# Within a weight unit: all K tiles of the first output tile, high and low weights in turn, then those of the second

## The chip, the cores and the metric

One core of a Trainium2 chip runs the whole program. The metric is the device time of one execution in microseconds (us). The kernel before takes 2347.33 us (median of 3 runs, 2344.61 to 2349.43).

## What is computed

A two-layer encoder trunk on 256 tokens of width 2048, in float32. Nearly all of the work is matrix products of the 256 token vectors with large weight matrices:

```python
for layer in range(2):
    x = x + (attention_layer if layer == 0 else rglru_layer)(rms_norm(x, g), ...)  # projections in and out
    x = x + memory_cross_attention(rms_norm(x, xa_norm[layer]), memn, wq, wkv, ...)
    x = x + conv_ffn(rms_norm(x, ffn_norm[layer]), w_up, conv_w, conv_b, w_down)   # 2048 -> 11264, 5632 -> 2048
```

## The kernel before

**Number format.** A float32 product is made from parts that TensorE takes in its fp32r format. ScalarE writes the high part of each weight (`w_hi`, L301), and VectorE writes the rest (`w_lo`, L307). Activations are split the same way into `xg_hl` or `a_hl`, which hold, for every K tile of 128 rows, 256 high columns and then 256 low columns. Three of the four partial products are computed: high weight with high and low activation, and low weight with high activation.

**Weight stream.** All weights are read from memory in 788 units of 128 x 1024 numbers, in the order of use, by SyncE's queue. There are four slots of `raw`, `w_hi` and `w_lo`. TensorE starts a unit when its `w_lo` is written (semaphore `lo_done`), and its last matmul signals `pe_unit`, upon which the slot is written again and, at the end of a block, the sums in PSUM are read.

**The unit that the diff touches.** 672 of the 788 units are "pair units" (`pair_unit`, which calls `pair_part`): four K tiles by two output tiles of 128 features. They make up the output projections (sections out0, xo0, down0, out1, xo1, down1), the up projections (up0, up1) and the recurrent block's input projection (rec). A K tile with one output tile takes two matmuls. The high one (L332) has 512 moving columns, the activation's high and low halves side by side, and fills a PSUM bank of 512 float32 columns. The low one (L336) has 256 moving columns and adds into the bank's second half. The two output tiles m = 0 and m = 1 have a bank each, `bank + m`. A block (one pair of output tiles, all its K tiles) uses banks 0 and 1 or 2 and 3 in turn. It begins with a wait on `proj_free`, the signal that the block before the last one has been read out.

**Waits inside a unit.** In the sections that start before all their inputs are split, `ready(xk)` waits for K tile xk: `tile_there` in `out_section`, and in the first block of `up_section` and `rec_section`. In xo0 and xo1 the first two blocks are issued in halves of two K tiles (`pair_part` with `ks` of length two), block 0 and block 1 in turn.

**The other two forms of unit** are not touched. `feature_unit` (L317, cross-attention queries) issues, for each K tile, three matmuls of 256 moving columns into the same half of one bank. `token_unit` (L352, attention and memory projections) has the activation as the stationary operand. For each K tile it issues three matmuls of mostly 512 moving columns into one bank and then three into a second bank.

Of the kernel before, what the change touches and what calls it, by code (L numbers as in the profile page):

```python
# [16 lines left out]
P = 128  # L17
# [60 lines left out]
def trunk(nc, t):  # L78
# [3 lines left out]
    with ctx:  # L82
# [11 lines left out]
        def sb(name, shape, dt=F):  # L94
            o = top[0]
            top[0] += size(shape)
            return at(name, o, shape, dt)
# [10 lines left out]
        w_hi = sb("w_hi", [SLOTS, UE], R)  # L108
# [85 lines left out]
        ps = ctx.enter_context(nc.psum_tensor("ps", [P, 8, COLS], F))  # L194
# [57 lines left out]
        n = 0  # L252
# [38 lines left out]
        def times(k, i, per):  # L291
            return k if i is None else k + i * per
# [28 lines left out]
        def pair_part(pe, c, k0, ks, x, bank, start, stop, i=None, per=0, ready=None, done=True):  # L321

            s = c % SLOTS
            pe.wait_ge(lo_done, times(c + 1, i, per))
            for k in ks:
                xk = k0 + k - ks[0]
                if ready:
                    ready(xk)
                both = x[:, xk, :, :].rearrange("p a n -> p (a n)")
                for m in range(2):  # L330
                    w = slice((2 * k + m) * P, (2 * k + m + 1) * P)
                    nc.tensor.matmul(ps[:, bank + m, :], w_hi[:, s, w], both, start=start and k == ks[0],  # L332
                                     stop=False, skip_group_check=True)
                for m in range(2):
                    w = slice((2 * k + m) * P, (2 * k + m + 1) * P)
                    last = nc.tensor.matmul(ps[:, bank + m, SEQ:2 * SEQ], w_lo[:, s, w], x[:, xk, 0, :], start=False,  # L336
                                            stop=stop and k == ks[-1], skip_group_check=True)
            if done:
                last.then_inc(pe_unit, 1)

        def pair_unit(pe, c, k0, x, bank, start, stop, i=None, per=0, ready=None):
            pair_part(pe, c, k0, range(4), x, bank, start, stop, i, per, ready)
# [139 lines left out]
        def _(pe):  # L482
# [143 lines left out]
            def out_section(name, ready, scale, base):  # L626
# [15 lines left out]
                if name == "out1":  # L642

                    for x, (q, u) in enumerate(OUT1_ORDER):
                        if u == 0:
                            pe.wait_ge(proj_free, fblock[name] + q + 1)
                        pair_unit(pe, c0 + x, 4 * u, a_hl, 2 * q, u == 0, u == units - 1, ready=tile_there)
                    blocks(None, (2, 3))
                    blocks(1, range(4))
                elif units == 1:  # L650

                    for q in range(2):
                        pe.wait_ge(proj_free, fblock[name] + q + 1)
                    for k in (0, 2):
                        for q in range(2):
                            pair_part(pe, c0 + q, k, (k, k + 1), a_hl, 2 * q, k == 0, k == 2, ready=tile_there, done=k == 2)
                    blocks(None, (2, 3))
                    blocks(1, range(4))
                else:
                    with pe.Fori(0, 2) as i:  # L660
                        blocks(i, range(4))
# [1184 lines left out]
```

## Time and profile before

| | |
|---|---|
| median of three runs | 2347.33 us (2344.61 to 2349.43) |
| profiled execution, its own time | 2346.71 us |
| its span, first to last instruction | 2345.0 us |
| mean granted TensorE clock | 0.998 |
| TensorE matmul busy | 2302.9 us, 98%, 13036 matmuls |
| TensorE weight load busy | 1997.7 us, 85% |
| VectorE busy | 1588.4 us, 68% |
| ScalarE busy | 1238.7 us, 53% |

PE is TensorE's matmuls, PEld its weight loads, DVE is VectorE, ACT ScalarE, POOL GpSimd, SP SyncE. A matmul's duration in a profile reaches from its start to its last result, so durations of neighbours overlap. The time that a matmul costs in a stream is the distance from its start to the start of the next one.

### The profile page before, as it was taken

The numbers are of one execution on the slowest core, as the hardware profiler recorded it, in microseconds if no ns is written. First come the engines' busy times: TensorE is split into PE (matmuls) and PEld (weight loads), VectorE is DVE, ScalarE is ACT, GpSimd is POOL, SyncE is SP. The second block draws the span as 40 slices with busy tenths as digits, with TensorE's granted clock in tenths as the row PEclk, the third lists the DMA queues.
The fourth block names the chain that finished last, engine by engine and source line by source line (L and its number), as shares of the span: only waits on it lengthen the run. The fifth ranks groups of instructions, "written<-read, shape, count | busy, mean of one in ns | idle before, by whom it ended". The sixth has DMA issues, their size and how long they took to land.

```text
span 2345.0 us, 38374 instructions
## 1 busy us (share of the span) xinstructions
PE 2302.9 (98%) x13036; PEld 1997.7 (85%) x13036; DVE 1588.4 (68%) x1968; ACT 1238.7 (53%) x1692; POOL 221.7 (9%) x207
## 2 busy tenths in 40 slices
PE   7999999999999999999999999999999999999999
PEld 6888878978888888888888888887888888888888
DVE  7766776576777777765555778667777777774444
ACT  5554555465555555544444776555555555553332
POOL 6630001130000000000000100212000000000000
PEclk9999999999999999999999999999999999999999
DMA  7565435545555555565555555534555555556554
GB/s 277 175 199 197 135 106 178 180 132 163 193 185 183 188 200 181 180 210 189 189 187 186 180 189 187 181 138 149 202 184 179 194 191 188 183 189 201 189 188 160
DMA packets 118077, 426.92 MB, mean 182 GB/s; under 512 B 13504, under 2 KB 14144, under 8 KB 117872
## 3 DMA queue, kind: packets, MB, share of 16 engines
q1 hardware_dynamic: 116640, 418.36, 53.5%
q0 software_dynamic: 1360, 7.52, 0.9%
q8 instruction: 50, 0.82, 0.1%
q14 instruction: 27, 0.22, 0.0%
HBM read 423.73 MB, written 2.10 MB: 182 GB/s over the span
## 4 chain that ended last, share of the span: by engine, by line
PE 89%; POOL 4%; issue 3%; DVE 2%; ACT 1%; DMA 1%; POOLq 0%; SPq 0%; ACTq 0%; DVEq 0%
PE ps L332 50%; PE ps L336 25%; PE ps L352 9%; PE ps L317 1%; POOL acc L405 1%; POOL sq L404 1%; PE ps L592 1%; PE ps L758 1%; POOL acc L1703 0%; DVE w_lo L307 0%; DMA memT<-in_mem_t 0%; POOL acc L1704 0%; PE ps L577 0%; ACT w_hi L301 0%; POOL rq L1644 0%
## 5 line engine op out<-in xcount | busy, mean ns | idle before, releaser
L307 DVE TENSOR_TENSOR w_lo<-raw,w_hi 128x1024 fp32r<-128x1024 f32 x788 | 963.8, 1244 | 514.1 <-ACT w_hi L301 510.8
L301 ACT ACTIVATE w_hi<-raw 128x1024 fp32r<-128x1024 f32 x788 | 811.9, 1054 | 593.1 <-PE ps L336 437.7
L332 PE MATMUL ps<-xg_hl,w_hi 128*128 128x512 f32 x3328 | 1047.8, 396 | 5.4 <-DVE w_lo L307 4.5
L336 PEld LDWEIGHTS ps<-xg_hl,w_lo 128*128 128x128 f32 x3328 | 625.9, 188 | 148.0
L336 PE MATMUL ps<-xg_hl,w_lo 128*128 128x256 f32 x3328 | 654.6, 278 | 0.0
L332 PE MATMUL ps<-a_hl,w_hi 128*128 128x512 f32 x2048 | 644.9, 396 | 8.3 <-DVE xT L1388 4.7
L332 PEld LDWEIGHTS ps<-xg_hl,w_hi 128*128 128x128 f32 x3328 | 507.6, 189 | 6.3 <-issue 4.8
L336 PEld LDWEIGHTS ps<-a_hl,w_lo 128*128 128x128 f32 x2048 | 384.7, 188 | 91.0
L336 PE MATMUL ps<-a_hl,w_lo 128*128 128x256 f32 x2048 | 402.4, 278 | 0.0
L332 PEld LDWEIGHTS ps<-a_hl,w_hi 128*128 128x128 f32 x2048 | 311.8, 189 | 11.2 <-DVE xT L1388 7.2
L1040 ACT ACTIVATE y_buf<-u_buf,fconv 128x256 f32<-128x256 f32 x176 | 96.4, 595 | 228.0 <-DVE u_buf L1470 228.0
L352 PE MATMUL ps<-w_hi,xg_hl 128*128 128x512 f32 (+1 forms) x576 | 174.3, 382 | 11.5 <-DVE w_lo L307 11.5
L1477 DVE SCALAR_TENSOR_TENSOR y_buf<-u_buf,fconv,y_buf 128x256 f32<-128x256 f32 x176 | 85.2, 485 | 82.2 <-ACT y_buf L1040 81.6
L352 PEld LDWEIGHTS ps<-w_hi,xg_hl 128*128 128x128 f32 x576 | 106.8, 189 | 33.3 <-issue 13.4
L352 PE MATMUL ps<-w_lo,xg_hl 128*128 128x512 f32 (+1 forms) x288 | 109.2, 379 | 0.0
L1515 DVE TENSOR_TENSOR u_buf<-cross,ps 128x512 f32<-128x512 f32 x88 | 60.5, 687 | 44.9 <-ACT cross L1073 44.9
L352 PE MATMUL ps<-w_hi,a_hl 128*128 128x512 f32 x256 | 86.1, 402 | 0.9 <-ACT kmem_tok L877 0.6
L1035 ACT ACTIVATE a_hl<-y_buf 128x512 f32 (+1 forms) x44 | 27.8, 632 | 104.1 <-DVE y_buf L1499 104.1
L1482 DVE SCALAR_TENSOR_TENSOR y_buf<-u_buf,fconv,y_buf 128x256 f32<-128x256 f32 x176 | 77.0, 479 | 0.2
L352 PEld LDWEIGHTS ps<-w_lo,xg_hl 128*128 128x128 f32 x288 | 54.7, 190 | 9.8
L1470 DVE TENSOR_TENSOR u_buf<-u_buf,r_bc 128x512 f32<-128x512 f32 x88 | 60.3, 685 | 0.0
L1026 ACT ACTIVATE y_buf<-y_buf 128x512 f32<-128x512 f32 x44 | 27.8, 633 | 61.2 <-DVE y_buf L1482 61.1
(186 smaller groups left out, 1414.8 us busy)
## 6 DMA issues: line engine op xcount, KB each, us to landing
raw<-in_w_stream SPq DMA_DIRECT2D x788, 512.0 KB, 3.9
bias<-in_rel_bias POOLq DMA_DIRECT2D x4, 768.0 KB, 6.0
memT<-in_mem_t POOLq DMA_DIRECT2D x1, 2048.0 KB, 11.0
gate_w<-in_gate_w POOLq DMA_DIRECT2D x4, 512.0 KB, 3.8
out_t<-xT SPq DMA_DIRECT2D x8, 256.0 KB, 4.4
xT<-in_x_t SPq DMA_DIRECT2D x2, 512.0 KB, 8.7
xT<-in_x_t SPq DMA_DIRECT2D x2, 384.0 KB, 6.0
xT<-in_x_t SPq DMA_DIRECT2D x1, 256.0 KB, 4.0
```

Of the source, the lines that this page charges most:

```text
L301: nc.scalar.activation(w_hi[:, s, :], raw[:, s, :], ACT.Copy).then_inc(hi_done, 1)
L307: nc.vector.tensor_tensor(w_lo[:, s, :], raw[:, s, :], w_hi[:, s, :].bitcast(F), ALU.subtract).then_inc(lo_done, 1)
L332: nc.tensor.matmul(ps[:, bank + m, :], w_hi[:, s, w], both, start=start and k == ks[0], stop=False, skip_group_check=True)
L336: last = nc.tensor.matmul(ps[:, bank + m, SEQ:2 * SEQ], w_lo[:, s, w], x[:, xk, 0, :], start=False, stop=stop and k == ks[-1], skip_group_ ...
L352: last = nc.tensor.matmul(ps[:, bank + tt, 0:n], a[:, k0 + k, tok], b[:, s, w], start=start and k == 0 and q == 0, stop=stop and k == nk - ...
L1026: A(flat(y_buf[:, 2:4, :]), flat(y_buf[:, 2:4, :]), ACT.Gelu_apprx_tanh).then_inc(gelu_done, 1)
L1035: A(pair_tiles(a_hi, 2 * half, 2, i, 4), y_buf[:, 0:2, :], ACT.Copy).then_inc(g_hi, 1)
L1040: A(y_buf[:, m, :], u_buf[:, m, 2:2 + SEQ], ACT.Identity, scale=column(fconv, w + 2, i, 32), bias=column(fconv, w + 3, i, 32)).then_inc(ta ...
L1470: V.tensor_tensor(part, part, r_bc[:, :].unsqueeze(1).to_broadcast([P, 2, SEQ]), ALU.mult).then_inc(u_scaled, 1)
L1477: middle.append(ch.mark(V.scalar_tensor_tensor(y_buf[:, m, :], u_buf[:, m, 1:1 + SEQ], column(fconv, 4 * (4 * half + m) + 1, i, 32), y_buf ...
L1482: ins = V.scalar_tensor_tensor(y_buf[:, m, :], u_buf[:, m, 0:SEQ], column(fconv, 4 * (4 * half + m), i, 32), y_buf[:, m, :], ALU.mult, ALU ...
L1515: V.tensor_tensor(u_buf[:, tile:tile + 2, 2:2 + SEQ], cross[:, :, :], ps[:, bank:bank + 2, 0:SEQ], ALU.add).then_inc(proj_free, 1)
```

## The change

Before, a K tile's four matmuls go high m=0, high m=1, low m=0, low m=1, and then the next K tile follows. Afterwards all K tiles of the part are done for m=0 (high, low, high, low, ...) and then all of them for m=1. The matmuls, their operands and their number stay the same. `ready` is called in the first pass only. The last matmul of the unit is the same one as before, and it carries the same signal.

```diff
             pe.wait_ge(lo_done, times(c + 1, i, per))
-            for k in ks:
-                xk = k0 + k - ks[0]
-                if ready:
-                    ready(xk)
-                both = x[:, xk, :, :].rearrange("p a n -> p (a n)")
-                for m in range(2):
+            for m in range(2):
+                for k in ks:
+                    xk = k0 + k - ks[0]
+                    if ready and m == 0:
+                        ready(xk)
                     w = slice((2 * k + m) * P, (2 * k + m + 1) * P)
-                    nc.tensor.matmul(ps[:, bank + m, :], w_hi[:, s, w], both, start=start and k == ks[0],
-                                     stop=False, skip_group_check=True)
-                for m in range(2):
-                    w = slice((2 * k + m) * P, (2 * k + m + 1) * P)
+                    nc.tensor.matmul(ps[:, bank + m, :], w_hi[:, s, w], x[:, xk, :, :].rearrange("p a n -> p (a n)"),
+                                     start=start and k == ks[0], stop=False, skip_group_check=True)
                     last = nc.tensor.matmul(ps[:, bank + m, SEQ:2 * SEQ], w_lo[:, s, w], x[:, xk, 0, :], start=False,
                                             stop=stop and k == ks[-1], skip_group_check=True)
```

## Rows read from the trace of the kernel before

**Rows 1.** The page: span, and busy time of each engine.
```profile
span 2345.0 us, 38374 instructions
PE 2302.9 (98%) x13036; PEld 1997.7 (85%) x13036; DVE 1588.4 (68%) x1968; ACT 1238.7 (53%) x1692; POOL 221.7 (9%) x207
```
**Rows 2.** The page: chain that ended last, shares by line.
```profile
PE ps L332 50%; PE ps L336 25%; PE ps L352 9%; PE ps L317 1%; POOL acc L405 1%; POOL sq L404 1%; PE ps L592 1%; PE ps L758 1%; POOL acc L1703 0%; DVE w_lo L307 0%; DMA memT<-in_mem_t 0%; POOL acc L1704 0%; PE ps L577 0%; ACT w_hi L301 0%; POOL rq L1644 0%
```
**Rows 3.** The page: groups; busy, mean ns of one, idle before, releaser.
```profile
L307 DVE TENSOR_TENSOR w_lo<-raw,w_hi 128x1024 fp32r<-128x1024 f32 x788 | 963.8, 1244 | 514.1 <-ACT w_hi L301 510.8
L301 ACT ACTIVATE w_hi<-raw 128x1024 fp32r<-128x1024 f32 x788 | 811.9, 1054 | 593.1 <-PE ps L336 437.7
L332 PE MATMUL ps<-xg_hl,w_hi 128*128 128x512 f32 x3328 | 1047.8, 396 | 5.4 <-DVE w_lo L307 4.5
L336 PE MATMUL ps<-xg_hl,w_lo 128*128 128x256 f32 x3328 | 654.6, 278 | 0.0
L332 PE MATMUL ps<-a_hl,w_hi 128*128 128x512 f32 x2048 | 644.9, 396 | 8.3 <-DVE xT L1388 4.7
L336 PE MATMUL ps<-a_hl,w_lo 128*128 128x256 f32 x2048 | 402.4, 278 | 0.0
```
**Rows 4.** Waits of PE: total us, times, longest.
```profile
PE ps L332 <- DVE xT L1388: 5.6, 14, 0.7
PE ps L332 <- DVE w_lo L307: 4.5, 2, 2.3
...
PE ps L332 <- DVE a_hl L1588: 2.5, 1, 2.5
...
PE ps L332 <- DVE a_hl L1329: 1.1, 1, 1.1
```
**Rows 5.** Timeline of PE in up0, at 799 to 806 us: start, length.
```profile
799.69 0.63 PE L332 MATMUL ps<-xg_hl,w_hi 128*128 128x512 f32 x2
800.15 0.40 PE L336 MATMUL ps<-xg_hl,w_lo 128*128 128x256 f32 x2
800.39 0.63 PE L332 MATMUL ps<-xg_hl,w_hi 128*128 128x512 f32 x2
...
805.26 0.62 PE L332 MATMUL ps<-xg_hl,w_hi 128*128 128x512 f32 x2
```
**Rows 6.** The same stretch in narrow windows: single matmuls and weight loads.
```profile
799.92 0.39 PE L332 MATMUL ps<-xg_hl,w_hi 128*128 128x512 f32 x1
800.16 0.19 PEld L336 LDWEIGHTS ps<-xg_hl,w_lo 128*128 128x128 f32 x1
800.27 0.28 PE L336 MATMUL ps<-xg_hl,w_lo 128*128 128x256 f32 x1
```
**Rows 7.** Windows of PE: stretch, length, busy (matmuls), granted clock, DMA share, GB/s.
```profile
548.00:551.50 3.50, 3.50 (x12) 0.55 0.70 193
600.00:1000.00 400.00, 400.00 (x2298) 1.00 0.56 188
...
1650.00:2050.00 400.00, 400.00 (x2298) 1.00 0.56 189
```
**Rows 8.** Timeline of PE in the token units: first and last triple of eleven.
```profile
164.83 0.62 PE L352 MATMUL ps<-w_hi,xg_hl 128*128 128x512 f32 x2
165.28 0.39 PE L352 MATMUL ps<-w_lo,xg_hl 128*128 128x512 f32 x1
...
171.63 0.62 PE L352 MATMUL ps<-w_hi,xg_hl 128*128 128x512 f32 x2
```
**Rows 9.** Chain in order of time, in the feature units: start, length.
```profile
446.50 14.40 PE ps L317 x120
```
**Rows 10.** Timeline of PE at 547.9 us, after a wait for weights.
```profile
547.94 0.82 PE L332 MATMUL ps<-xg_hl,w_hi 128*128 128x512 f32 x2 [2.18 <-DVE w_lo L307]
548.56 0.63 PE L336 MATMUL ps<-xg_hl,w_lo 128*128 128x256 f32 x2
548.98 1.05 PE L332 MATMUL ps<-xg_hl,w_hi 128*128 128x512 f32 x2
549.84 0.63 PE L336 MATMUL ps<-xg_hl,w_lo 128*128 128x256 f32 x2
```
**Rows 11.** Timeline of DVE and PE where out0 starts.
```profile
356.25 1.29 DVE L1329 TENSOR_TENSOR a_hl<-oT,a_hl 128x512 fp32r<-128x512 f32 x2 [0.45 <-ACT a_hl L939]
357.09 0.69 PE L332 MATMUL ps<-a_hl,w_hi 128*128 128x512 f32 x2 [1.08 <-DVE a_hl L1329]
```
**Rows 12.** Timeline of DVE where xo0 and up0 start.
```profile
482.94 0.42 DVE L1436 TENSOR_TENSOR a_hl<-ps,a_hl 128x256 fp32r<-128x256 f32 x1 [0.93 <-ACT a_hl L992]
483.89 0.42 DVE L1436 TENSOR_TENSOR a_hl<-ps,a_hl 128x256 fp32r<-128x256 f32 x1 [0.53 <-ACT a_hl L992]
...
514.80 0.98 DVE L1158 SCALAR_TENSOR_TENSOR xg_hl<-xT,gains,xg_hl  x2
```
**Rows 13.** Timeline of PE where xo0 starts, its third block, and where up0 starts.
```profile
483.09 0.81 PE L332 MATMUL ps<-a_hl,w_hi 128*128 128x512 f32 x2
...
486.06 0.63 PE L332 MATMUL ps<-a_hl,w_hi 128*128 128x512 f32 x2
...
489.25 0.73 PE L332 MATMUL ps<-a_hl,w_hi 128*128 128x512 f32 x2 [0.24 <-DVE xT L1388]
...
510.12 0.73 PE L332 MATMUL ps<-xg_hl,w_hi 128*128 128x512 f32 x2 [0.45 <-DVE xT L1388]
```

## The prediction, made before the changed kernel was run

> **What bounds the kernel now.** I read the page's busy times first. Matmuls keep TensorE busy for 2302.9 of 2345.0 us, and the next engine, VectorE, has 1588.4 [rows 1]. Then I read the shares of the chain that ended last: three quarters of it are the two matmul lines that the diff reorders, L332 and L336 [rows 2]. The groups of the page show the same from the other side. The two engines that prepare weights stand idle for 514.1 and 593.1 us, and ScalarE's idle time ends mostly on L336, so the weights wait for TensorE and not the reverse [rows 3]. The idle time in front of L332 is 5.4 + 8.3 us, in front of L336 it is nothing [rows 3]; who ended it is in the waits, of which the largest is the readout of a block (L1388), 14 times and 5.6 us together [rows 4]. So the time is the number of matmuls times the distance between their starts. Only a change of that distance can move the total by much.
>
> **How many matmuls.** The diff reorders 3328 + 2048 = 5376 high matmuls and as many low ones [rows 3], 10752 together, 16 in each of the 672 pair units. A distance that changes by 0.1 ns per matmul is 1.1 us in the total. The bound for telling a change from none, 0.2%, is 4.7 us, which is 0.44 ns per matmul.
>
> **The distance now.** From 799.69 to 805.26 us eight K tiles start, 32 matmuls [rows 5]: 5.57 / 32 = 174.1 ns each, or 0.696 us for the four of a K tile. Two windows of 400 us agree, with 2298 matmuls each [rows 7]: 800 / 4596 = 174.1 ns. Within a K tile the starts are 799.69 (high), 799.92 (high), 800.15 (low), 800.27 (low), 800.39 (the next high) [rows 5, 6]. A high one therefore takes 0.23 us whether a high or a low one comes next, and a low one takes 0.12 us whether a low or a high one comes next. That is the heart of the forecast: to the 10 ns of these rows, the distance goes by the length of the matmul itself and not by its neighbour. The rows can't resolve 0.44 ns, though, so the order could still matter at the scale that decides.
>
> **What the change removes.** It removes the change of bank after each matmul and, with it, the two adjacent low matmuls. It removes no instruction: all 10752 matmuls keep their operands, and each still loads its own weights.
>
> **What it adds, first: each matmul adds into the bank that the one before it has just written.** The other two unit forms do this already. The feature units put 256-column matmuls one after another into the same columns of one bank: 120 of them in 14.40 us, 120.0 ns each [rows 9]. The token units put three 512-column ones into one bank, then three into another: from 164.83 to 171.63 us ten triples start [rows 8], 6.80 / 30 = 226.7 ns each, the same for every triple. Neither is slowed by the same bank. 120.0 + 226.7 = 346.7 ns for one of each, against 696 / 2 = 348 ns for a high and a low one in the stream that alternates banks. So staying in a bank costs nothing there; it is cheaper, if anything, by some 0.7 ns per matmul (174.1 against 173.35).
>
> **Second: high and low alternate.** A weight load takes 0.19 us, longer than a low matmul's 0.12 us, and starts with the matmul before the one it serves [rows 6]. Eight loads of a unit start under a high matmul and eight under a low one, before as after. Before, the two under the lows follow each other at once; afterwards each has a long matmul on both sides. If loads were what stretches the low matmuls, this would help. But the feature units load weights under nothing but 256-column matmuls and still take 120.0 ns [rows 9], and the 512-column ones of the token units, which cover a load fully, have the same surplus: 226.7 - 512 / 2.4 = 13.4 ns and 120.0 - 256 / 2.4 = 13.3 ns. At 1.2 GHz, the clock's lower level, which was granted at 549 us, the surplus is gone: four matmuls from 548.98 take two distances of 0.43 and two of 0.21 us (0.86 to the first low at 549.84) [rows 10], which is 512 / 1.2 and 256 / 1.2. So the surplus is a fixed amount per matmul beside the columns, and is not the load. I take nothing for this part.
>
> The Trainium skill gives a distance for this surplus ("TensorE: Matmul & The Clock Gate", section "Back-to-back issue gap"): the columns at 2.4 GHz plus about 2.5 ns. By that a K tile's four matmuls would take 650 ns in either order; the trace has 696. The rule has no term for the order or the bank, and its number does not hold here.
>
> **Bounds of the unknown.** The trace has no stream in which 512 and 256 columns alternate one by one. The stream of before has, per K tile, two steps between lengths and four changes of bank, and it costs about 0.7 ns per matmul more than the pure streams do on average. If the surplus comes from the changes of bank, it goes away: -0.7 x 10752 = -7.7 us. If it comes from the steps between lengths, these double from two to four per K tile, and it doubles: +7.7 us. If it belongs to each matmul in a mixed stream, nothing changes. Against the first stands that the token units change bank after every third matmul without a mark on it. Against the second stands that the high ones take 0.23 us with either neighbour. I take the middle, 0.
>
> **Third: the waits for K tiles come closer together.** The fourth tile of a unit is now needed after 6 matmuls (1.04 us) instead of 12 (2.09 us). This could stall TensorE only where a section begins. In out0 the first two pairs of tiles are written by 356.25 + 1.29 = 357.54 us, and TensorE starts at 357.09 [rows 11]; tile 2 is needed at 357.09 + 0.70 = 357.79, so 0.25 us are left. In xo0, split in halves, heads 2 and 3 are written at 483.36 and 484.31 [rows 12], and their matmuls start at 486.06 [rows 13]. Up0 starts at 510.12 [rows 13]; its last two tiles are written by 515.78 [rows 12], and tile 14 is needed three units later, at 510.1 + 8.4 + 0.7 = 519.2. Layer 1 repeats this. These waits cost nothing; if out0's cover were gone, it would be 0.35 us once. Behind a waiting matmul only TensorE's own queue stands, and no DMA is issued by it.
>
> **What stays.** The unit's last matmul still signals, so slots are freed, weights fetched and banks read at the same points. In the xo sections TensorE waits for VectorE's readout (L1388) [rows 4, 13], whatever its own order; the 16 units there would neither gain nor lose in full. The 1.1 and 2.5 us waits for a_hl are at a section's or unit's start.
>
> **Clock.** After the wait of 2.18 us that ends at 547.94 us [rows 10] the clock was at the lower level for most of 3.5 us, 0.55 on average [rows 7], which cost 3.5 x 0.45 = 1.6 us. The change does not touch that wait. The Trainium skill (same page, section "A second HAM failure mode: psum-queue depth-cycling") says that cycling through banks can make the engine idle so often that its clock falls and rises, which would speak for this change. In this kernel the clock was 1.00 in both long windows with full bank cycling [rows 7], so there is nothing of the kind to win back.
>
> **Sum.** 0 (neighbour) + 0 (bank) + 0 (waits) = 0. The profiled execution took 2346.71 us and its span was 2345.0, with 1.7 us around it; the median of the runs is 2347.33, 0.6 above. The forecast goes by the median: 2347.3 us, and its own range is 2343 to 2352.
>
> **Rivals.**
> 1. *Each step between lengths costs.* If a switch between 512 and 256 columns leaves a bubble, there are 16 of them per unit instead of 8. Price +7.7 us: 2355 us, slower. It decides once a step costs over 0.9 ns (4.7 us / 5376 added steps). For it: pure streams, both of them, are cheaper than the mixed one. Against it: no neighbour effect in rows of 10 ns. Chance 0.30.
> 2. *Bank changes cost, and go.* -7.7 us: 2339.6 us, faster. For it: the pure streams are also those that stay in a bank. Against it: the token units' second triple. Chance 0.22.
> 3. *A sum in the same bank must wait for the one before it,* since the low matmul adds to columns that the high one wrote last. It would have to show in the feature units, which write the same 256 columns every time, and does not. If it cost 13 ns (a whole surplus) at each low matmul it would be 5376 x 13 = 70 us: 2417 us. Chance 0.03.
> 4. *Loads are eased.* If a low matmul fell to its bare 256 / 2.4 = 107 ns, 5376 x 9 = 48 us would go: 2299 us. The fixed surplus speaks against it. Chance 0.02.
> The rest, 0.43, is the forecast.
>
> **How the numbers follow.** The two rivals near the forecast lie at 2339.6 and 2355; with 2 to 3 us for the runs' own spread (2344.61 to 2349.43) the range is 2337 to 2358. It leaves out rivals 3 and 4 and some tails. Faster by over 0.2%: rival 2, rival 4 and a little of the forecast's edge, 0.26. Slower: rivals 1 and 3, 0.34. Within 0.2%: 0.40.
>
> **What would show it.** In the changed kernel's timeline of up0, starts at 0, 0.23, 0.35, 0.58, 0.70 us, and 2298 matmuls, give or take 1, in a 400 us window; rival 1 would give some 2289 and rival 2 some 2307. The waits of PE should keep their list, with L1388 first at about 5.6 us, and no new wait on L1329, L1436 or L1158. What would make the forecast wrong is a distance that hangs on the neighbour by more than 0.44 ns per matmul, which no row of before can exclude, or a new clock drop.

## The result: slower, by an amount that differs from run to run

The changed kernel takes 2367.61 us (median of 5 runs, 2353.7 to 2370.21) and the kernel before 2346.41 us (5 runs, 2344.61 to 2349.43). The ratio on record is 1.008, with a 95% interval of 1.0053 to 1.0107 (it and the ratios below are not the quotients of the two medians, which is 1.009 here). The forecast was 2347.3 us with a range of 2337 to 2358. The runs of the changed kernel spread over 16.5 us, those of the kernel before over 4.8 us.

The profiled execution is the one of 2353.7 us. Its page, changed kernel: header, busy times, chain by line and the groups that answer to [rows 1 to 3]. L331 is now the high matmul and L333 the low one.

```profile
span 2352.0 us, 38374 instructions
PE 2310.9 (98%) x13036; PEld 2001.0 (85%) x13036; DVE 1589.6 (68%) x1968; ACT 1238.7 (53%) x1692; POOL 221.1 (9%) x207
...
PE ps L331 50%; PE ps L333 25%; PE ps L349 9%; PE ps L317 1%; POOL acc L402 1%; POOL sq L401 1%; PE ps L589 1%; PE ps L755 1%; POOL acc L1700 0%; DMA memT<-in_mem_t 0%; DVE w_lo L307 0%; POOL acc L1701 0%; PE ps L574 0%; ACT w_hi L301 0%; POOL rq L1641 0%
...
L331 PE MATMUL ps<-xg_hl,w_hi 128*128 128x512 f32 x3328 | 1167.7, 397 | 5.3 <-DVE w_lo L307 4.4
```

The shape of the profile is that of before. TensorE's busy time has grown by 8.0 us, from 2302.9 to 2310.9. The idle time in front of the high matmuls of this group is 5.3 us against 5.4 [rows 3]. The waits of PE in the changed kernel are those of [rows 4]: total us, times, longest.

```profile
PE ps L331 <- DVE xT L1385: 5.5, 14, 0.7
...
PE ps L331 <- DVE w_lo L307: 4.4, 2, 2.2
PE ps L331 <- DVE a_hl L1585: 2.6, 1, 2.6
```

So there is no new wait. The time went into the distance between matmuls, and it did so in some stretches only. Windows of PE in the changed kernel (stretch, length, busy with number of matmuls, granted clock, DMA share, GB/s), beside [rows 7]:

```profile
600.00:1000.00 400.00, 400.00 (x2266) 1.00 0.55 184
...
1700.00:2000.00 300.00, 300.00 (x1733) 1.00 0.56 190
```

From 600 to 1000 us there are 2266 matmuls where the kernel before has 2298: 176.5 ns each instead of 174.1. From 1700 to 2000 us there are 1733, 173.1 ns each, which is less than before. Both stretches are up projections with the same code, the clock is 1.00 in both, and TensorE is busy throughout. Single matmuls (timeline of PE, changed kernel: start, length), first in the long cadence and then in the short one:

```profile
800.03 0.40 PE L331 MATMUL ps<-xg_hl,w_hi 128*128 128x512 f32 x1
800.26 0.28 PE L333 MATMUL ps<-xg_hl,w_lo 128*128 128x256 f32 x1
800.38 0.40 PE L331 MATMUL ps<-xg_hl,w_hi 128*128 128x512 f32 x1
...
801.09 0.40 PE L331 MATMUL ps<-xg_hl,w_hi 128*128 128x512 f32 x1
```

```profile
1320.09 0.39 PE L331 MATMUL ps<-xg_hl,w_hi 128*128 128x512 f32 x1
...
1321.13 0.39 PE L331 MATMUL ps<-xg_hl,w_hi 128*128 128x512 f32 x1
```

Three high-low pairs take 1.06 us in the first (800.03 to 801.09) and 1.04 us in the second (1320.09 to 1321.13). Call the mean time of a pair unit of 16 matmuls over an unbroken stretch its level. The starts in the trace give two levels and hardly any other: 2773.3 ns, the short level, and 2826.7 ns, the long level (at the long level single units take 2820, 2827 and 2833 ns in turn, since its pattern of starts repeats every three pairs and a unit has eight). The kernel before has one, 2786.7 ns, in every stretch of its 640 units that run unbroken. In the profiled execution of the changed kernel 300 such units are at the long level and 339 at the short one. That accounts for the time: 300 x 40.0 - 339 x 13.4 = 12.0 - 4.5 = 7.5 us, and the execution is 2353.7 - 2346.4 = 7.3 us over the median of before. The other four executions, 22.0 us over it on average, would need some 580 of the 672 units at the long level (an estimate: 672 x 13.4 = 9.0 us has to be lost too, and (22.0 + 9.0) / 0.0534 = 580).

The question is then why a stream of high and low matmuls in turn has two levels, whether the bank has a part in it, and what picks the level.

### The profile page after: what moved, and what is told of

Read it like the earlier page. It is cut to its first block, busy times and chain, and to the rows that moved or that the text cites. A ratio compares the mean times of both kernels' runs of the same rounds, so it can differ in the third digit from the quotient of the medians.

```text
span 2352.0 us, 38374 instructions
## 1 busy us (share of the span) xinstructions
PE 2310.9 (98%) x13036; PEld 2001.0 (85%) x13036; DVE 1589.6 (68%) x1968; ACT 1238.7 (53%) x1692; POOL 221.1 (9%) x207
## 4 chain that ended last, share of the span: by engine, by line
PE 89%; POOL 4%; issue 3%; DVE 2%; ACT 1%; DMA 1%; POOLq 0%; SPq 0%; ACTq 0%; DVEq 0%
PE ps L331 50%; PE ps L333 25%; PE ps L349 9%; PE ps L317 1%; POOL acc L402 1%; POOL sq L401 1%; PE ps L589 1%; PE ps L755 1%; POOL acc L1700 0%; DMA memT<-in_mem_t 0%; DVE w_lo L307 0%; POOL acc L1701 0%; PE ps L574 0%; ACT w_hi L301 0%; POOL rq L1641 0%
## 5 line engine op out<-in xcount | busy, mean ns | idle before, releaser
L331 PE MATMUL ps<-xg_hl,w_hi 128*128 128x512 f32 x3328 | 1167.7, 397 | 5.3 <-DVE w_lo L307 4.4
L333 PE MATMUL ps<-xg_hl,w_lo 128*128 128x256 f32 x3328 | 929.1, 279 | 0.0
L331 PEld LDWEIGHTS ps<-xg_hl,w_hi 128*128 128x128 f32 x3328 | 625.3, 188 | 155.7 <-issue 5.0
L331 PE MATMUL ps<-a_hl,w_hi 128*128 128x512 f32 x2048 | 719.1, 397 | 8.2 <-DVE xT L1385 4.5
L333 PEld LDWEIGHTS ps<-xg_hl,w_lo 128*128 128x128 f32 x3328 | 627.7, 189 | 0.1
L333 PE MATMUL ps<-a_hl,w_lo 128*128 128x256 f32 x2048 | 571.3, 279 | 0.0
L331 PEld LDWEIGHTS ps<-a_hl,w_hi 128*128 128x128 f32 x2048 | 384.3, 188 | 104.1 <-DVE xT L1385 8.4
L333 PEld LDWEIGHTS ps<-a_hl,w_lo 128*128 128x128 f32 x2048 | 385.7, 188 | 0.1
L1070 ACT ACTIVATE cross<-ps 128x512 f32<-128x512 f32 x104 | 60.1, 578 | 0.0
```

The costliest lines, as they stand in the source:

```text
L331: nc.tensor.matmul(ps[:, bank + m, :], w_hi[:, s, w], x[:, xk, :, :].rearrange("p a n -> p (a n)"), start=start and k == ks[0], stop=False ...
L1070: A(cross[:, :, :], ps[:, bank:bank + 2, SEQ:2 * SEQ], ACT.Copy).then_inc(cross_ready, 1)
```

## The experiments

The numbers in ns per unit below are distances between the starts of matmuls in each kernel's own profile, where units run unbroken. "Pure sum" means 226.7 ns for each 512-column matmul and 120.0 for each 256-column one [rows 8, 9]; it is 2773.3 ns for a unit. The short level of the changed kernel is exactly that, but only as a sum: in it a high matmul takes 230.8 or 232.3 ns and a low one 112.8 or 117.4, so the single distances are not those of the pure streams.

### The same kernel again

No edit. In the diffs from here on `high(k, m)` and `low(k, m)` stand for the two matmul calls of the changed kernel, L331 and L333, and the calls of `ready` are left out.

> The changed kernel once more. In its first profile a pair unit took either 2.773 us or 2.825 us (mean over three units), whole stretches at a time, and the level changed only where TensorE had stalled. Theory A (the level is drawn anew at each stall): the two levels come back, but in other stretches, and the time is anywhere from 2346 - 672 x 0.013 = 2337 us to 2346 + 672 x 0.039 = 2372 us. Theory B (the level goes with the place in the program): the same stretches as in the first profile, 2353 us.

One run, 2354.24 us. Both levels came back, in partly different stretches. The first 23 unbroken units of the first up projection, at 550 us, are now at 2773.3 ns, where they were at 2826.7. The four longer stretches of the recurrent block's input projection, from 1302 us on, are short, long, short, short in both profiles. Neither theory holds as it was put: some places repeat, others differ. The most telling spot is where the level changed without any stall that the waits show. Timeline of PE, and then of its weight loads, in this run:

```profile
613.44 0.28 PE L333 MATMUL ps<-xg_hl,w_lo 128*128 128x256 f32 x1
613.56 0.39 PE L331 MATMUL ps<-xg_hl,w_hi 128*128 128x512 f32 x1
613.79 0.28 PE L333 MATMUL ps<-xg_hl,w_lo 128*128 128x256 f32 x1
613.91 0.45 PE L331 MATMUL ps<-xg_hl,w_hi 128*128 128x512 f32 x1
614.19 0.28 PE L333 MATMUL ps<-xg_hl,w_lo 128*128 128x256 f32 x1
```

```profile
613.56 0.19 PEld L333 LDWEIGHTS ps<-xg_hl,w_lo 128*128 128x128 f32 x1
613.85 0.19 PEld L331 LDWEIGHTS ps<-xg_hl,w_hi 128*128 128x128 f32 x1
```

A load normally starts with the low matmul it runs under. Here the low one starts at 613.79 and the load at 613.85, 0.06 us late, and the next high matmul takes 0.28 us instead of 0.23 until the next start. From then on the stream is at the long level for 231 unbroken units, through the rest of up0 and down0: one slip of 0.05 us, and 40 + 13 = 53 ns more in each unit after it.

The trace shows where this slip comes from. The late load is the first one of a unit, and that unit's `w_lo` is written only just before. Timeline of VectorE in the same run:

```profile
612.57 1.23 DVE L307 TENSOR_TENSOR w_lo<-raw,w_hi 128x1024 fp32r<-128x1024 f32 x1 [0.21 <-ACT w_hi L301]
```

VectorE ends at 613.80, and the load follows 0.05 us later (54 ns; the shortest such distances in this profile and in five others are 52 to 54 ns). So this is a wait for weights, too short to stand in the list of waits. In the first profile, at the long level, the same load came 0.21 us after its weights and not late. The run with the highs' weights halved (below) changes its level twice inside the up projections, at 612.3 and 1668.8 us, and both times at a first load that is 0.06 us late and comes 0.05 us after its weights. The short level uses the weights up faster, so it is likely to meet such a wait sooner; that is argued and was not tested.

### Alternation without the single bank

```diff
-            for m in range(2):
-                for k in ks:
+            for k in ks:
+                for m in range(2):
                     high(k, m)
                     last = low(k, m)
```

> Only the alternation of high and low: per K tile high 0, low 0, high 1, low 1, so the bank changes after every second matmul as it doesn't in the changed kernel. Theory A (length changes after each matmul make the second level): both levels, 2773 and 2825 ns per unit, time 2337 to 2372 us. Theory B (eight matmuls into one bank make it): one level as before, 2787 ns, 2346 us, or 2773 ns, 2337 us.

2360.39 us (median of 10 runs, 2342.1 to 2369.65), ratio 1.0042 (1.0015 to 1.0068). Windows of PE in this kernel:

```profile
600.00:1000.00 400.00, 400.00 (x2267) 1.00 0.55 184
1300.00:1330.00 30.00, 30.00 (x174) 1.00 0.58 193
...
1700.00:2000.00 300.00, 300.00 (x1701) 1.00 0.55 184
```

1701 matmuls in 300 us, where the changed kernel had 1733 in the same window of the program. Both levels are there (2773.3 and 2826.7 ns), and the runs spread over 27 us. Theory A as expected; eight matmuls into one bank are not needed.

### The single bank without alternation

Eight matmuls into one bank, in the order high, high, low, low of two K tiles.

```diff
             for m in range(2):
-                for k in ks:
-                    high(k, m)
-                    last = low(k, m)
+                for a, b in zip(ks[::2], ks[1::2]):
+                    for k in (a, b):
+                        high(k, m)
+                    for k in (a, b):
+                        last = low(k, m)
```

> Only the bank: eight matmuls into one bank, but in the order high, high, low, low of two K tiles. Theory A (alternation of lengths): 2787 ns per unit everywhere, 2346 us, no difference. Theory B (one bank): two levels again, or if a bank change costs, 2773 ns and 2337 us.

2346.12 us (median of 10 runs, 2344.53 to 2350.19), ratio 1.0001 (0.9992 to 1.0011), and 2786.7 ns in every stretch:

```profile
600.00:1000.00 400.00, 400.00 (x2299) 1.00 0.56 188
```

In this order the bank costs nothing and gives nothing. Theory A. One combination was not run: high and low in turn with a change of bank after every matmul. In the changed kernel and in the one above each low matmul adds into the bank that the high one before it wrote. That the bank has no part in the alternating order either is argued from this run and not shown.

### Longer runs of one length

First all eight highs of a unit and then its eight lows, banks in turn; then, in one bank, four highs and four lows.

```diff
-            for m in range(2):
-                for k in ks:
-                    high(k, m)
-                    last = low(k, m)
+            for k in ks:
+                for m in range(2):
+                    high(k, m)
+            for k in ks:
+                for m in range(2):
+                    last = low(k, m)
```

```diff
             for m in range(2):
                 for k in ks:
                     high(k, m)
+                for k in ks:
                     last = low(k, m)
```

> All eight high matmuls of a unit and then all eight low ones, banks in turn. Two steps between lengths per unit instead of 8 (before) or 16 (changed). Theory A: the surplus of a mixed stream goes with the steps, so a unit takes 8 x 226.7 + 8 x 120.0 = 2773 ns or little more, everywhere, and the time is 2346 - 672 x 0.013 = 2337 us, in every run. Theory B (banks): the bank changes after each matmul, so at least 2787 ns, 2346 us or more.

> One bank for eight matmuls, four highs and then four lows. From the measured streams of 1, 2 and 8 in a row: two and two cost 3.3 ns over the pure sum per high-low cycle, eight and eight cost 20 ns. Theory A (one level for each pattern, the surplus is paid at the steps between lengths): one level, between 2773 + 2 x 3.3 = 2780 and 2773 + 2 x 20 = 2813 ns per unit, hence 2342 to 2364 us, the same in all runs. Theory B (banks): one bank for eight gives two levels, as in the changed kernel.

Eight and eight: 2352.04 us (9 runs), ratio 1.0026 (1.0015 to 1.0036), 2793.3 ns. Four and four: 2358.28 us (4 runs), ratio 1.0049 (1.0033 to 1.0066), 2806.7 ns, with one short stretch of five units at 2800.0. Windows of the two, in this order:

```profile
600.00:1000.00 400.00, 400.00 (x2294) 1.00 0.56 187
```

```profile
600.00:1000.00 400.00, 400.00 (x2282) 1.00 0.55 186
```

The expectation for eight and eight was a miss of 20 ns per unit. Fewer steps between lengths do not mean a smaller surplus: over the pure sum the units are at 0 or 53 ns with 16 steps, 13 ns with 8 (the kernel before), 33 ns with 4, and 20 ns with 2. After a step to the highs, the first five of them take 5 to 6 ns more than 226.7 on average (eight and eight), and the first two lows after a step take 7 and 1 ns less than 120.0. "A bubble per step", my first rival, is thereby wrong as a rule. These values and the two levels are all multiples of 6.67 ns.

### Is it the lengths, or the kind of matmul?

The low matmul of the changed kernel with 512, 384 and 192 columns instead of 256.

```diff
-  ps[:, bank + m, SEQ:2 * SEQ],   w_lo[:, s, w], x[:, xk, 0, :]
+  ps[:, bank + m, :],             w_lo[:, s, w], x[:, xk, :, :].rearrange("p a n -> p (a n)")             # 512
+  ps[:, bank + m, P:2 * SEQ],     w_lo[:, s, w], x[:, xk, :, :].rearrange("p a n -> p (a n)")[:, 0:3 * P]  # 384
+  ps[:, bank + m, SEQ:SEQ + 192], w_lo[:, s, w], x[:, xk, 0, 0:192]                                        # 192
```

> The changed order, same bank for eight, but the low matmul has 512 moving columns too (it adds the product of low weight and low activation, which the kernel otherwise leaves out). So the kind of weights still alternates, and the length doesn't. If the alternation of lengths makes the levels: 16 x 226.7 = 3627 ns per unit in every stretch, one level. If it is the alternation of high and low weights, or the bank, or the loads alone: more than 3627 ns in some stretches. The time is about 2346 + 672 x 0.840 = 2911 us.

> The changed order, but the low matmul has 384 moving columns instead of 256 (it also adds half of the low weight times low activation, into columns 128 to 511, so the output isn't the reference's). A pure stream would give 226.7 + 173.3 = 400 ns for a pair, 3200 ns for a unit. Theory A1 (any one-by-one alternation of two lengths has a second cadence): units of 3200 ns in some stretches and of some 3250 in others. Theory A2 (the second cadence comes about because a low matmul of 256 columns, 120 ns, is just as long as the load of the next weights): the load now has 50 ns to spare, and every stretch is at 3200 ns.

> The changed order, but the low matmul has 192 moving columns (it leaves out the low weights' product for the last 64 tokens). If the columns alone set its distance, it takes 93.3 ns and a unit takes 8 x (226.7 + 93.3) = 2560 ns, with or without a second level. If the load of the next weights, which runs under it, sets the floor (theory A2's premise), it stays at 120 ns, and a unit stays at 2773 ns, with or without the second level at 2827 ns.

Each of the three kernels was run once. With 512 columns: 2890.86 us, and 3626.7 ns in every stretch, the pure sum. High and low weights still alternate, in one bank, each with its load; with equal lengths there is one level and no surplus. With 384: 2662.05 us, and two levels again, 3306.7 and 3253.3 ns, 107 and 53 ns over the pure sum of 3200. Windows of PE with 512 columns, and then with 384:

```profile
650.00:1050.00 400.00, 400.00 (x1767) 1.00 0.45 145
```

```profile
600.00:1000.00 400.00, 400.00 (x1938) 1.00 0.48 157
1900.00:2300.00 400.00, 400.00 (x1969) 1.00 0.49 162
```

Here a low matmul takes 175 ns until the next start, some 55 ns more than before, over the same load. So theory A2, that the low one is just as long as a load, is not what makes two levels. With 192 columns: 2324.26 us, levels of 2720.0 and 2755.5 ns, neither 2560 nor 2773. Timeline of PE and then of its loads with 192 columns:

```profile
699.90 0.25 PE L333 MATMUL ps<-xg_hl,w_lo 128*128 128x192 f32 x1
699.99 0.41 PE L331 MATMUL ps<-xg_hl,w_hi 128*128 128x512 f32 x1
700.24 0.25 PE L333 MATMUL ps<-xg_hl,w_lo 128*128 128x192 f32 x1
```

```profile
699.90 0.19 PEld L331 LDWEIGHTS ps<-xg_hl,w_hi 128*128 128x128 f32 x1
700.01 0.19 PEld L333 LDWEIGHTS ps<-xg_hl,w_lo 128*128 128x128 f32 x1
```

The low one's distance falls to 0.09 us, but the load for the low one that follows starts 0.02 us after its high matmul, and 0.11 us after the load before it. In the pair units of this run 5348 of the loads start 108 or 109 ns after the one before, and none sooner, and the high matmul makes up for it (0.25 us). So here the loads do bind: of the 26.7 ns that 64 columns fewer take off the pure sum of a pair, the better level saves only 6.7 (2773.3 to 2720.0 ns per unit). Fewer than 192 columns were not tried.

### What part do the loads have?

64 instead of 128 weight columns are loaded and multiplied. The cut shows the high matmul; the low one is cut in the same way. Which matmuls that holds for, and what the kernels leave out, the expectations say.

```diff
+                    n = P if k == ks[0] else P // 2        # highs: whole only in a unit's first K tile
+                    w = slice((2 * k + m) * P, (2 * k + m) * P + n)
-                    nc.tensor.matmul(ps[:, bank + m, :], w_hi[:, s, w], ...
+                    nc.tensor.matmul(ps[0:n, bank + m, :], w_hi[:, s, w], ...
```

> The changed order with 512 and 256 moving columns, but in three of four K tiles only 64 of the 128 weight columns are loaded and multiplied (half of the output features get only the first K tile of each unit). Theory A2 (load as long as the low matmul): the loads are half as long, and units are at 2773 ns or a little under it everywhere. Theory A1 (alternation of lengths): two levels, 2773 and about 2827 ns, as in the changed kernel.

> The changed order, with only the low weights' loads cut to 64 of 128 columns (the low product is left out for half of the output features). These loads run under the high matmuls, 227 ns long, where they are hidden anyway. With all loads but each unit's first highs halved, there was one level, 2760 ns. If the load under the short matmul is what makes the second level, both levels stay here, 2773 and 2827 ns. If loads of either kind do, the second level goes, or shrinks to half.

> The changed order, with only the high weights' loads cut to 64 of 128 columns in three of four K tiles (the high products are left out for half of the features there). These loads run under the low matmuls, 120 ns long. If the load under the short matmul makes the second level, there is one level here, at 2773 ns or a little under it. If loads of either kind do, the second level stays or shrinks to half.

> The kernel before (high, high, low, low), with 64 of 128 weight columns loaded and multiplied in three of four K tiles (the rest is left out). With whole loads a unit takes 2787 ns. If the surplus over the columns' own 2560 ns comes with the loads in this order too: one level, well under 2787 ns, about the 2760 ns that the changed order showed with half loads. If the loads are hidden in this order: 2787 ns as before.

| halved | order | time, us (one run) | levels, ns per unit |
|---|---|---|---|
| none | high, low | 2353.7 to 2370.21 | 2773.3 and 2826.7 |
| both | high, low | 2329.3 | 2760.0 |
| lows | high, low | 2334.43 | 2720.0 and 2773.3 |
| highs | high, low | 2329.12 | 2746.7, and in part 2773.3 |
| none | high, high, low, low | 2346.41 | 2786.7 |
| both | high, high, low, low | 2352.8 | 2793.3 |

Windows of PE with both halved in the changed order, and then in the order before:

```profile
600.00:1000.00 400.00, 400.00 (x2320) 1.00 0.56 189
```

```profile
600.00:1000.00 400.00, 400.00 (x2294) 1.00 0.56 187
```

With both halved in the changed order the second level is gone, and the one that remains is below the short one. With only the lows halved, whose loads run under the long matmuls and seemed hidden, the two levels seen are 2720.0 ns (53 units) and 2773.3 (the rest), each 53 ns below one of the changed kernel's and still 53 ns apart. This 2773.3 is not the old short level: a high matmul takes 229.2 ns and a low one 117.5, in every pair alike. So narrower weights move the levels, those of the low matmuls too. In the order before they cost 7 ns per unit. No theory on record had that.

Each of these kernels changes two things at once: the load, which takes 135 ns instead of 188, and the matmul, which fills only 64 output columns. No run changes one without the other. That it is the load which moves the levels is likely, since the 192-column run shows loads binding, but it is not shown.

### What picks the level?

An extra matmul of 2, 128 or 256 columns at the start of each block, whose result is overwritten. There are 152 such blocks (the instructions grow by 304, a matmul and a load each); the expectation's 168 was a miscount.

```diff
+                    if start and m == 0 and k == ks[0]:
+                        nc.tensor.matmul(ps[:, bank, 0:N], w_hi[:, s, w], x[:, xk, 0, 0:N], start=True, stop=True,
+                                         skip_group_check=True)
```

> The changed kernel with one extra matmul of two columns at the start of each of the 168 + 0 blocks of pair units (its result is overwritten), so that the stream is disturbed every 1, 4 or 11 units and not only where TensorE stalls. If any disturbance draws the level anew: both levels, changing from block to block, and the time of the runs spreads less than that of the changed kernel (some 17 us there), around the middle of the levels, 2355 us plus what the extra matmuls cost (blocks x 0.06 to 0.12 us, some 12 to 20 us). If the level goes with the place in the program and not with the disturbance: the long stretches stay at one level.

> The changed kernel with the extra matmul at the start of each block 128 columns long instead of 2. With two columns, 112 of 120 stretches with more than two whole units were at 2827 ns. If the level after a disturbance goes by how far it shifts the stream: another share, up to all stretches at 2773 ns. If a slow stream stays slow whatever hits it: nearly all at 2827 ns again.

> The same with 256 columns, so that at each block's start two 256-column matmuls follow one another. If two of a length in a row let the stream fall in step anew: a share of fast stretches unlike that with two columns (8 of 120). If a slow stream stays slow whatever hits it: nearly all at 2827 ns.

Of the stretches with at least three unbroken units in each profile, 8 of 126 are at the short level with 2 columns, 42 of 127 with 128, and 122 of 127 with 256. The times are 2383.56 us (4 runs, ratio 1.0164, 1.0147 to 1.0181), 2375.84 and 2354.82 us. So a disturbance does not draw the level at even odds; in these profiles, one of each kernel, the share goes by its length. Windows of PE with 2 and with 256 columns (the extra matmuls counted):

```profile
600.00:1000.00 400.00, 400.00 (x2280) 1.00 0.54 184
```

```profile
600.00:1000.00 400.00, 400.00 (x2320) 1.00 0.55 186
```

The last kernel's extra matmuls cost 152 x 0.12 = 18 us; without them its time would be near 2337 us, the short level's.

That suggested three orders without extra work: the changed order, but with the first K tile of each block, or of each unit, going high, high, low, low; and with high and low swapped for the second output tile.

```diff
+            for k in ks[:1] if start else ():        # e16; e17: in every unit
+                high(k, 0); high(k, 1); low(k, 0); low(k, 1)
             for m in range(2):
-                for k in ks:
+                for k in ks[1:] if start else ks:
                     high(k, m)
                     last = low(k, m)
# e18
+            for k in ks:
+                high(k, 0); low(k, 0)
+            for k in ks:
+                low(k, 1); last = high(k, 1)
```

> The changed order, except that each block's first K tile goes high, high, low, low as before. No work is added. If two lows in a row, as the 256-column disturbance made them, let the stream fall into the fast level: nearly all stretches at 2773 ns, 2346.3 - 672 x 0.0133 = 2337.4 us plus some 3.3 ns in each of 152 blocks, 0.5 us: 2338 us, and the same in all runs. If it was the disturbance and not the pair: both levels, 2340 to 2370 us, as the changed kernel.

> The same in every unit: the first K tile of each unit high, high, low, low, then the rest high and low in turn. If pairs reset the stream to the fast level and each pair of pairs costs the 3.3 ns that it costs in the order before: 2776.7 ns per unit, 2346.3 - 672 x 0.010 = 2339.6 us, the same in all runs. If the cost of mixing goes by the pattern otherwise: one level somewhere between 2773 and 2827 ns.

> The changed order with high and low swapped for the second output tile: per unit one pair of lows (between the tiles) and one pair of highs (between units), four pairs of steps apart. If a pair of lows resets to the fast level and a pair of highs disturbs it: a level between, or both within a unit; 2773 to 2800 ns. If any pair of one length resets it: 2773 to 2777 ns, 2337 to 2340 us, the same in all runs.

None brought the short level throughout: 2357.5 us (5 runs, ratio 1.0051, 1.0038 to 1.0065), 2354.37 us (6 runs, 1.0034, 1.0022 to 1.0046) and 2361.96 us (4 runs, 1.0067, 1.0052 to 1.0082). The first has both levels, as its second expectation says. The second alternates between units of 2777 and 2817 ns. The third takes mostly 2805 and 2815 in turn, 2810 on average, above anything expected of it. The first two show how the level moves. Timeline of PE, one high pair per block in the first up projection (L327 is the high matmul there, L332 the low one):

```profile
693.37 0.63 PE L327 MATMUL ps<-xg_hl,w_hi 128*128 128x512 f32 x2
...
704.67 0.63 PE L327 MATMUL ps<-xg_hl,w_hi 128*128 128x512 f32 x2
...
715.76 0.63 PE L327 MATMUL ps<-xg_hl,w_hi 128*128 128x512 f32 x2
...
727.06 0.63 PE L327 MATMUL ps<-xg_hl,w_hi 128*128 128x512 f32 x2
```

Blocks take 11.30, 11.09 and 11.30 us in turn. A block is one high, high, low, low group (0.696 us in the trace) and 30 pairs: at the long level 0.696 + 30 x 0.3533 = 11.30, at the short one 0.696 + 30 x 0.3467 = 11.10. Here the group switches the stream to the other level every time. In the variant with one group per unit it does so too, every unit: two units take 2 x 0.6965 + 6 x (0.3467 + 0.3533) = 5.593 us, 2796.5 each, and 2796.6 was measured. In the down projection of e16, whose blocks have 86 pairs between groups, the stream stays at the long level across the groups. A reading that fits is that what a group does depends on where it falls in the long cadence, whose pattern of starts repeats every three pairs: 30 and 6 pairs are multiples of three, and 86 is not. It fits three cases and was not tested by itself.

## Why the prediction was wrong

- **What bounds the kernel** was right: no wait changed, and the whole difference is the distance between matmuls.
- **"The distance goes by the length of the matmul itself and not by its neighbour"** was the failing step. I read it from starts in one steady pattern, at 10 ns, and carried it to a pattern that the trace did not have. It did not hold even in the trace of before: averaged over the unbroken units, a high matmul takes 233 ns there and a low one 115, against 226.7 and 120.0 in the pure streams. In the new pattern a pair takes 346.7 or 353.3 ns, against 348.3 before. The forecast's 0 ns occurs in neither.
- **The bounds of the unknown** failed with it. I took the mixed stream's surplus over the pure ones, 0.7 ns per matmul (the starts give 13.4 / 16 = 0.84), and let it vanish or double: 2339.6 or 2355 us. The lower end was nearly the size of the short level (13.4 x 672 = 9.0 us under the median). The upper end was too small: the long level is 2.5 ns per matmul over the kernel before, 40 x 672 = 27 us, where I had 7.7. With all units long the time would be 2373 us; the measured runs reach 2370.21.
- **Rival 1** (steps between lengths) had the right cause in part, since equal lengths show no surplus, but the wrong law: two and four steps per unit cost more than eight. **Rival 2** (bank changes) had the sign and size of the short level for the wrong reason: the bank by itself moved nothing, 1.0001 (0.9992 to 1.0011). **Rival 3** (a sum in the same bank waits) is excluded by the same run. **Rival 4** was priced wrongly: from 120.0 to 107 ns are 13.3 ns and not 9, 71 us and not 48. No run took it that far.
- **"So the surplus is a fixed amount per matmul beside the columns, and is not the load"** was wrong in its first half as far as a mixed stream goes: the surplus there is 0 to 53 ns per unit, by order and stretch. The second half is in doubt. Halved weights (load and output columns together) moved the unit from 2773.3 and 2826.7 to 2760.0 ns with both halved, and by 53 ns with the lows' alone. What held in both pure streams did not hold between them.
- **The waits for K tiles** at 0, and the clock without a term, were right: the rows of waits are the same, and the clock is 1.00 in the windows.
- **No run-to-run spread** was allowed for beyond that of before. One slip of 0.05 us can switch the changed kernel's cadence for hundreds of microseconds, so its time is a mixture.

What stays open is the mechanism inside TensorE that ties loads and matmuls of unequal length into these rhythms, and what sets the level after an ordinary stall. Shown is that two levels come with matmuls of unequal length in turn and not with equal ones, that narrower weights move them, that the bank has no part in the order of before, and that a level is kept for up to 254 units on end and can be changed by a slip of 0.05 us. None of the orders tried beats the kernel before in every run. The changed order itself would at its short level (an estimate, 2346.4 - 9.0 = 2337 us), but nothing tried here without extra work keeps it there.

## What to carry to other kernels

A stream of matmuls can have more than one steady cadence. Where matmuls of two lengths are mixed, pure streams of each do not bound the mixture from above, and an order that the trace does not have needs a run. If the runs of a kernel spread more than those of its sister with the same work, compare the number of matmuls in equal windows of one profile before looking for a wait. The order high, high, low, low gave up 13 ns per unit against the best case and in return had the same time in every stretch, which was the better bargain.

## What the runs showed of the hardware that was not expected

- 512 and 256 moving columns in turn, each with its own load of 128 columns: 346.7 or 353.3 ns per pair, at a granted clock of 1.00, for up to 254 units on end. Equal lengths of 512, high and low weights in turn: 226.7 ns each in all unbroken units of the one profile.
- The mean unit times of most orders with 512 and 256 columns and full loads are multiples of 6.67 ns: 2773.3, 2786.7, 2793.3, 2800.0, 2806.7, 2826.7. One group per unit (2796.6) and the second tile low first (2810) fit only over two units.
- In the pair units no two weight loads of 128 columns started closer together than 0.11 us, and with a low matmul of 192 columns most of those under it did so at 0.108 to 0.109 us. Halving the low weights, whose loads run under the 512-column matmuls and look hidden, took 53 ns off a unit (load and output columns halved together).
- Halving the weights, load and output columns, can make a stream slower: 2786.7 to 2793.3 ns in the order before.
- A unit's first load came 0.06 us late, 0.05 us after its weights were written, and the stream went from the short to the long level for the next 231 unbroken units.
